# Small expert passes in raw fp32: 64 stationary tokens on each of the two column halves

## The reference, cut to what matters

```python
def moe_swiglu(h, w_router, w1, w3, w2):
    logits = (h @ w_router).astype(jnp.float32)
    top_logit, top_idx = lax.top_k(logits, TOP_K)
    gates = jax.nn.softmax(top_logit, axis=-1)
    ...
    def expert_block(args):
        xblk, e = args
        return (jax.nn.silu(xblk @ w1[e]) * (xblk @ w3[e])) @ w2[e]
    ...
    return jnp.zeros_like(h).at[tok].add(yb * gate[:, None])
```

## Time and profile before

| | us |
|---|---|
| median of 3 runs (2659.92 to 2661.28) | 2660.08 |
| profiled execution, span and own time | 2660.3 |
| PE busy | 2579.5 (97%) |
| DVE busy | 1747.8 (66%) |
| ACT busy | 1376.6 (52%) |
| pass 0 (small), from PE's first product to pass 1's | 1664 to 1774 |
| passes 1 and 2 (wide) | 1774 to 2109.5 |
| passes 3 to 7 (small) | 2109.5 to 2633 |
| output rows, last scatter, final norm, output | 2633 to 2660.3 |

### The profile page before, as it was taken

One profiled execution on the slowest core, in us unless ns is written; L12 is line 12 of the kernel. 1 busy time (PEld: TensorE's weight loads), 2 busy tenths in 40 slices (PEclk: granted clock), 3 DMA queues, 4 the chain that ended last, 5 costly groups with the idle time before them and its releaser, 6 DMA issues. The chain is left out here.

```text
span 2660.3 us, 46550 instructions
## 1 busy us (share of the span) xinstructions
PE 2579.5 (97%) x18338; PEld 2049.6 (77%) x18338; DVE 1747.8 (66%) x2600; ACT 1376.6 (52%) x2029; POOL 0.2 (0%) x4
## 2 busy tenths in 40 slices
PE   8999999999999999999999999999999999999997
PEld 6787777888788888877877899678888866666665
DVE  4876575445422233357765667977659899898897
ACT  5534375223422222255344635765557777777775
POOL 0000000000000000000000000000000000000000
PEclk9999999999999999999999999999999999999998
DMA  7011274224222223210103455885569999999996
GB/s 292 2 51 33 79 262 152 95 95 167 80 95 95 95 95 131 102 68 2 51 33 127 161 184 195 347 365 206 206 247 344 363 404 423 417 422 417 416 422 277
DMA packets 74103, 533.20 MB, mean 200 GB/s; under 512 B 8128, under 2 KB 9536, under 8 KB 9536
## 3 DMA queue, kind: packets, MB, share of 16 engines
q1 hardware_dynamic: 73632, 528.84, 51.3%
q10 hardware_dynamic: 288, 1.74, 0.2%
HBM read 529.50 MB, written 1.05 MB: 199 GB/s over the span
## 5 line engine op out<-in xcount | busy, mean ns | idle before, releaser
L1711 ACT ACTIVATE arena<-bank 128x512 f32<-128x512 f32 (+6 forms) x564 | 267.0, 489 | 724.6 <-PE bank L610 651.5
L1711 ACT ACTIVATE weights_high<-ring 128x1024 fp32r<-128x1024 f32 (+1 forms) x332 | 442.8, 1342 | 269.7 <-PE bank L610 255.7
L2533 DVE TENSOR_TENSOR weights_low<-ring,weights_high 128x1024 fp32r<-128x1024 f32 x220 | 266.8, 1224 | 400.6 <-ACT weights_high L1711 400.5
L610 PE MATMUL bank<-h_low,weights_high 128*128 128x512 f32 (+1 forms) x960 | 347.3, 362 | 0.0
L2930 DVE TENSOR_TENSOR weights_low<-ring,weights_high 128x2048 fp32r<-128x2048 f32 x112 | 255.7, 2286 | 53.5 <-ACT weights_high L1711 53.2
L610 PE MATMUL bank<-arena 64*64 64x64 f32 (+5 forms) x4944 | 266.9, 242 | 15.6 <-DVE arena L2748 4.5
L610 PEld LDWEIGHTS bank<-arena 64*64 64x64 f32 (+3 forms) x4944 | 224.5, 143 | 39.1 <-issue 13.9
L610 PEld LDWEIGHTS bank<-h_low,weights_high 128*128 128x128 f32 x960 | 182.0, 190 | 27.3
L2930 DVE TENSOR_TENSOR more_weights_low<-arena,weights_high 128x2048 fp32r<-128x2048 f32 x78 | 178.3, 2286 | 30.3 <-ACT weights_high L1711 29.5
L610 PE MATMUL bank<-h_high_gates,weights_high 128*128 128x512 f32 (+1 forms) x512 | 173.1, 338 | 4.3 <-DVE weights_low L2533 3.6
L610 PE MATMUL bank<-h_high_ffn,weights_high 128*128 128x512 f32 x448 | 175.7, 392 | 1.4 <-DVE h_low L2540 0.8
(11 more groups left out here) (384 smaller groups left out, 5123.0 us busy)
## 6 DMA issues: line engine op xcount, KB each, us to landing
ring<-wstream SPq DMA_DIRECT2D x345, 1024.0 KB, 5.2
arena<-wstream SPq DMA_DIRECT2D x153, 1024.0 KB, 8.3
xT<-xin SPq DMA_DIRECT2D x2, 1024.0 KB, 6.2
cn<-consts SPq DMA_DIRECT2D x1, 1576.0 KB, 21.2
sm<-small SPq DMA_DIRECT2D x1, 1568.0 KB, 23.6
sm<-small ACTq DMA_DIRECT2D x1, 1568.0 KB, 10.8
out<-hT SPq DMA_DIRECT2D x2, 512.0 KB, 3.0
cn<-consts ACTq DMA_DIRECT2D x1, 130.0 KB, 3.0
```

The costliest lines, as they stand in the source:

```text
L610: return nc.tensor.matmul(o, lhsT, rhs, start=first, stop=last)
L1711: return nc.scalar.activation(o, i, func, **kw)
L2533: step(vx.tensor_tensor(ring_low[:, u % RING, cols], ring[:, u % RING, cols], wh[:, j % 4, :].bitcast(F32), ALU.subtract), "weights low", j)
```

## The change

In small passes no unit is split, and neither are tokens and hidden. The 64 slots are one fp32 stationary operand of 64 columns (`xs`, `gs`), and `small_unit` multiplies a raw unit with four matmuls: of an inner unit the even k-tiles go to output rows 0 to 63 and the odd ones to rows 64 to 127, which is the left and the right half of the array's columns; of a down unit the two hidden tiles do. The two halves of the rows are then partial sums, and the steps that added them before add them still. The hidden is turned from its 64 rows alone. `first_high`, `next_high` and the low parts for a small pass are gone; a wide pass after a small one still gets its first three units copied, which ACT does when they have landed. At the end three units of a pass that may not come are loaded, instead of four. Wide passes are as before.

```diff
-UNSPLIT = [2] + list(range(7, 2 * PAIRS, 4)) + [33, 38]
-SPLIT = [q for q in range(MOE_UNITS) if q not in UNSPLIT]
...
+        xs = nc.alloc_sbuf_tensor_at("tokens", [P, KD, SMALL], F32, offset=tile_at(8))
+        gs = nc.alloc_sbuf_tensor_at("hidden", [P, FT, SMALL], F32, offset=tile_at(14))
...
-            begun = SPLIT[AHEAD - 1] + 1
+            begun = AHEAD
...
+                def small_unit(q, factors):
+
+
+                    pe.wait_ge(moe_loaded[q % MOE_RING], i * (16 * MOE_UNITS // MOE_RING) + 16 * (q // MOE_RING + 1))
+                    for o, left, cols, first, last in factors:
+                        ins = mm(o, left, moe_slot(q)[0][:, cols], first, last)
+                    ins.then_inc(*tick(moe_used, kind, "spent", q))
+
                 def by_unit(q, factors, low_done, more=(), more_room=()):
...
-                    if not wide:
-                        for o, left, cols, first, _ in factors:
-                            mm(o, left[0], high[:, cols], first, False)
-                        pe.wait_ge(*low_done)
-                        for o, left, cols, _, last in factors:
-                            ins = mm(o, left[0], low[:, cols], False, last)
-                        return ins.then_inc(*tick(moe_used, kind, "spent", q))
...
+                        o, h = bank[5 - 3 * (p % 2)][:, c * P:c * P + to.stop], ghid[to, p % 2, c * P:(c + 1) * P]
+                        ins = nc.tensor.transpose(o, h, C("ident")) if wide else mm(o, h, C("ident", SMALL)[to, :])
...
+                            small_unit(q, [(bank[3 + p % 2][rows(k), :], xs[:, 4 * b + k, :], slice(k * TOK, (k + 1) * TOK),
+                                            b == 0 and k < 2, b == 1 and k >= 2) for k in range(4)])
...
+                        small_unit(2 * PAIRS + q, [(bank[6 + n][rows(c), :], gs[:, 2 * q + c, :],
+                                                    slice(c * D + n * 512, c * D + n * 512 + 512), q == 0, q == PAIRS - 1)
+                                                   for n in range(2) for c in range(2)])
...
-            first_high(AHEAD - 1)
...
                 def next_high(q):
 
-                    u = split_units(wide_next)[q]
-                    act.wait_ge(moe_loaded[u], (i + 1) * (16 * MOE_UNITS // MOE_RING) + 16)
-                    act.wait_ge(*here("spent", split_units(wide)[q - AHEAD]))
-                    f(moe_high(q), moe_slot(u)[0], ACT.Copy).then_inc(*tick(e_scalars, kind, "next high", q))
+                    if not wide_next:
+                        book.leave_out(e_scalars)
+                        return
+                    act.wait_ge(moe_loaded[q], (i + 1) * (16 * MOE_UNITS // MOE_RING) + 16)
+                    if wide:
+                        act.wait_ge(*here("spent", MOE_UNITS + q - AHEAD))
+                    f(moe_high(q), moe_slot(q)[0], ACT.Copy).then_inc(*tick(e_scalars, kind, "next high", q))
...
-                    if l and t == KD - 2:
-                        dve.wait_ge(*done("first high", 0))
-                        rest(0)
...
                 for q in range(AHEAD - 1):
+                    if not wide_next:
+                        book.leave_out(e_vectors)
+                        continue
                     dve.wait_ge(*here("next high", q))
-                    rest(split_units(wide_next)[q], q).then_inc(*tick(e_vectors, kind, "next low", q))
+                    rest(q).then_inc(*tick(e_vectors, kind, "next low", q))
```

More of the change, by code:

```diff
@@ L505, in in_pass @@
             return s, (i + 1) * per_pass(s) + value
-        BOUNDARY = [("y kept", 0), ("y kept", 1), ("gathered low", 0), ("gathered low", 1)] + \
+        BOUNDARY = [(name, b) for name in ("y kept", "gathered kept", "gathered low") for b in range(2)] + \
             [(name, q) for name in ("next high", "next low") for q in range(AHEAD - (name == "next low"))]
@@ L1530, in before, with hidden_ready @@
                     return in_pass(i - 1, *step)
+                def hidden_ready(p):
+                    return here("hidden low" if wide else "hidden kept", p)
+                def small_unit(q, factors):
[3 more added lines that the diff above has]
+                    ins.then_inc(*tick(moe_used, kind, "spent", q))
                 def by_unit(q, factors, low_done, more=(), more_room=()):
                     low = moe_slot(q)[1]
[L1536 to L1549 removed]
+                    high = moe_high(q)
+                    pe.wait_ge(*(here("high", q) if q >= AHEAD else before("next high", q)))
                     for o, left, cols, first, _ in factors:
@@ L1590, in expert_pass @@
                         if q == 0:
-                            pe.wait_ge(*before("gathered low", 1))
+                            pe.wait_ge(*before("gathered low" if wide else "gathered kept", 1))
                             if full:
@@ L1646, in expert_pass @@
                     if q == 0:
-                        pe.wait_ge(*here("hidden low", PAIRS - 5))
+                        pe.wait_ge(*hidden_ready(PAIRS - 5))
                         if full:
@@ L2333, in expert_pass @@
                     next_high(q)
-                act.wait_ge(*here("next high", AHEAD - 1))
-                f(es[:, 3:4], V("eps"), ACT.Copy)
+                act.wait_ge(*(here("next high", AHEAD - 1) if wide_next else here("y high", 1)))
+                f(es[:, 3:4], V("eps"), ACT.Copy).then_inc(*tick(e_scalars, kind, "pass left"))
                 pass_end(e_scalars, kind)
@@ L2925, in attention, with rest @@
                         weights_low(LAYER_START[l] + min(weights_due(l, n), GATE_AT + 4))
-            def rest(q, turn=None):
+            def rest(q):
                 raw, low = moe_slot(q)
-                return vx.tensor_tensor(low, raw, moe_high(q if turn is None else turn).bitcast(F32), ALU.subtract)
+                return vx.tensor_tensor(low, raw, moe_high(q).bitcast(F32), ALU.subtract)
             def scaled_router():
@@ L3092, in _ @@
             step(pick_tokens(0, False), "first picked")
-            vx.memset(ptg[:, :].bitcast(F32), 0.0)
-            for q in range(1, AHEAD - 1):
-                dve.wait_ge(*done("first high", q))
-                rest(q)
-            for b in range(2):
-                dve.wait_ge(*done("first kept", b))
-                step(vx.tensor_tensor(xh[:, 4 * b:4 * b + 4, SMALL:SLOTS],
-                                      bank[b][:, 0:4 * SMALL].rearrange("p (k t) -> p k t", k=4),
-                                      xh[:, 4 * b:4 * b + 4, 0:SMALL].bitcast(F32), ALU.subtract), "first low", b)
+            step(vx.memset(ptg[:, :].bitcast(F32), 0.0), "slot rows cleared")
             own()
-            dve.wait_ge(*done("first high", AHEAD - 1))
             dve.sem_inc(e_vectors, per_pass(e_vectors))
@@ L3233, in low @@
                     dve.wait_ge(*here("high", q))
-                    rest(q, high_turn(q, wide)).then_inc(*tick(e_vectors, kind, "low", q))
+                    rest(q).then_inc(*tick(e_vectors, kind, "low", q))
                 def add_last(g):
```

120 lines of the change are left out of this document (50 added, 70 removed).

## The result

| | median, us | lowest to highest | runs |
|---|---|---|---|
| before | 2660.0 | 2658.4 to 2661.3 | 4 |
| with the change | 2637.8 | 2636.0 to 2639.6 | 4 |
| with the change, a second time | 2636.7 | 2635.5 to 2639.1 | 4 |

The ratio to the kernel before is 0.9913, with an interval of 0.990 to 0.9925 (the second time 0.9907, 0.989 to 0.9923, against 2660.8). Faster by 22 us; the forecast was 2636.4.

The account below looks back on a forecast made before the run. The prediction took DMA to bound four small passes, PE passes 1 and 2, and the split to count only in pass 0, pass 3's front and the tail. 13.4 + 3.2 + 7.1 = 23.7 us gave 2636.4 us, range 2626 to 2646.

Parts of the forecast that it names:

- What bounds the passes: Small passes: DMA alone sets four of them, 2.50 us per unit; the split counts in pass 0, pass 3's front, the tail.
- PE per unit: PE in small passes: a changed unit takes 0.86 us with halves side by side, 1.71 us in turns.
- Rival 3: Small passes: PE becomes the bound, with halves in turns and a low clock, about 3050 us; chance 0.04.
- Start of pass 0: Before pass 0's first product: a subtraction and the tokens' low half fall away, 0.8 and 0.6 us gained.
- Pass 0: First small pass: loading resumes at 1664.6 us at the saturated rate, last unit lands at 1754.6, 13.4 us gained with the start.
- Pass 0 to pass 1: From pass 0's last unit to pass 1: copy, subtraction, rows and hand-over take 10.0 us, against 10.1 before.
- So nothing is given back: Boundary from pass 0 to pass 1: the 13.4 us gained by then stay.
- The clock: Small passes and tail: PE half idle may lose full clock; passes stay under 105 us, tail's unit 0.9 us more, 2637.3.
- Passes 1, 2 and 3: Passes 1 and 2 are PE's, gain 0; pass 3 rises from 406 to 419 GB/s, gain 3.2 us.
- passes 4 to 7: Last four small passes: gain 0, because DMA is full.
- rival 1: Small passes: DMA gets faster once ACT and DVE leave the weights alone, 12.9 us more, 2623.5 us; chance 0.09.
- Tail: From pass 7's last unit to the last scatter: 3.6 us instead of 10.7, through ACT's and DVE's rows, gain 7.1 us.

Follow-up runs that it names:

- half loads: Changed kernel, with passes 3 to 7 loading only the first half of each weight unit and multiplying it twice: 2570.0 us (one run).
- the warm end: Changed kernel with one loop, rows between the copies, 12 + 6 added matmuls after pass 0, 8 + 4 + 4 + 4 at the end: 2628.7 us.

## Why the prediction was right, step by step

*What bounds the passes.* "In four of them nothing but DMA counts": right. 42 loads of 1 MB (44.0 million bytes) at 422 GB/s are 104.4 us, passes with half the products keep that time, and passes with half the loads leave it. "75 us of 105" for PE's units before is 33 x 1.81 + 9 x 3.41 = 90 us, and 102 with its other work; "36 + 14 = 50 us" after is 90: the factor of two in a raw unit, as the runs with 12 raw units and with half loads show. The sum didn't notice, as 90 is still under 104.4. For pass 0 the record blamed the split's path through ACT, DVE and PE. That reading failed too: PE was busy for 106.6 of 110 us, and its waits for DVE's low parts come to 2.7 us of the 103 from 1665 to 1768. With 12 raw units, so with three fewer to copy and subtract, pass 0 took 2.8 us more: 112.5 us from its first product to pass 1's (1661.52 to 1774.04) for 109.7 (1664.65 to 1774.34). So it was mostly PE's products that set pass 0, and it gains because PE's work falls from 102 to 90 us.

*PE per unit.* "If they run side by side": right, and worth 72 us of PE's time per pass. Both ends of the bound were mispriced: 0.86 and 1.71 us were written, and 1.71 and 3.41 measured. With it falls "either value is under 2.50 us, and the choice moves only the tail": in turns the kernel is 337 us slower than before. Rival 3 asked for two failures where the first alone was enough, so its chance was put too low.

*Start of pass 0.* 1.7 for 1.4. DMA resumes 2.13 us after the first product (1659.74 to 1661.87) where 1.35 was said: the unit's price again.

*Pass 0.* 9.8 for 12.0. The rate is the saturated one, as forecast, but for the first loads. Missing are 0.8 us at the start (above) and 1.4 behind it: from the resumed issue to the last unit's products it is 91.4 us, not 90.0. By the transfers' records the first load lands 5.4 us after its issue (5.0 forecast), the other 34 take 85.9 us (85.0 forecast, as two of the first three come 0.4 to 0.6 us late), and PE takes up the last one 0.1 us after it has landed.

*Pass 0 to pass 1.* The chain was right to 0.2 us (9.8 for 10.0). The step that failed is "So nothing is given back": what stands behind the chain runs at half clock, which costs 2.4 us (1.6 in the second execution). "The clock" looked for this loss in the tail and in the passes, where PE's waits are 0.55 us and the clock stays at 1.00, not at the boundary, where PE waits 2.55 and 2.17 us. The Trainium skill ("TensorE: Matmul & The Clock Gate", HAM oscillation) warns of matmul bursts between waits for DMA, and has a case with long bursts that keeps the clock. The boundary agrees with the warning (clock 0.50 after a wait of 2.55 us), and passes 3 to 7 are like the long bursts: 0.55 us of waiting in each 2.49, and the clock at 1.00. The forecast had put them under the warning because it took PE for half idle.

*Passes 1, 2 and 3.* 0 for passes 1 and 2 is right to 0.1 us. By the transfers' records the last unit of pass 2 lands 12.5 us earlier than before, that of pass 3 14.9 and that of pass 7 17.9. So pass 3 gains 2.4 us for 3.2, and *passes 4 to 7* gain 3.0 for 0: "0, DMA is full" gave away the difference between 419 and 422 GB/s, 105 x (1 - 419 / 422) = 0.75 us per pass. It isn't rival 1: before reaches 422 in good stretches too,

```profile
2242.00:2292.00 50.00, 49.77 (x210) 34.12 (x209) 46.07 (x52) 40.05 (x49) 0.00 (x0) 1.00 1.01 422
```

so ACT and DVE don't slow the transfers. Before, PE and DVE, each within some us of the limit, sometimes freed a slot late; that is argued from the rows, no run took it apart.

*Tail.* 3.4 + 1.2 for 7.1. The step that failed is the path: the forecast led it through ACT's and DVE's rows, and PE's idle time of the earlier trace rows, put down to DVE's rows, hid a jump of 5 us that already ended last. After the change PE reaches the jump sooner, 1.10 us after the last unit was taken up instead of 5.41, and the jump takes 0.95 us longer: 3.4 us are left. Without the jump it is 3.70 us, for 3.6 forecast, but that is luck in part: the last unit's products took 1.94 us where 0.2 + 0.86 + 0.17 was said, and one half of DVE's rows was enough, 0.75 us, where both were counted, 1.4. After the scatter, 1.2 us came that the sum left out. ACT's last copy for the pass that never comes (2637.16, 1.91 us) had also held back the squares for the final norm: they started 1.5 us after the first residual (2640.43 to 2641.91) and start 0.5 us after it now (2618.70 to 2619.22).

So the total was right in good part because errors cancelled: 9 us too much in pass 0 (2.2), at the boundary (2.2), in pass 3 (0.8) and in the tail (3.7), against 8 too little at the start (0.3), in passes 4 to 7 (3.0), behind the scatter (1.2) and in a profiled execution of before that had lost 3.2 us to the clock. Behind that loss the two traces differ by 19.3 us, and by 20.8 with the second execution of the changed kernel. Whether the executions without a profile lost as much there isn't known; the medians differ by 22.2 us. The terms of the stated range add up to 7.8 and 9.4 us, where 9.6 and 10.4 were used; the result lies within either.

## What to carry to other kernels

Count instructions per unit of work from a group's total over a whole pass, not from a burst in the timeline, above all where one line of the program can issue two; a price off by two can hide for as long as something else sets the time, and takes every "it would still fit" with it. When work is cut from beside a saturated queue, the gain lies at the ends of the saturated stretch, and what is late next there can stand in no engine's row: here a jump, and the clock after a longer wait. A view names one releaser; where two waits end within half a microsecond, as DVE's rows and the jump did before the change, look at both. Look behind the last wait for both, and test a margin by halving the load of whatever sets the time, which shows how far the next limit is away.

## What the runs showed of the hardware

- An fp32 product in this trace is two matmul instructions of 0.43 us per 512 columns each; two column halves with moving data of their own ran side by side at no loss (89.7 against 161.7 us per pass, which is 1.71 us less for each unit of 3.41).
- On PE a branch to the head of a loop or out of its end took 0.08 to 0.25 us, one over the block of passes that don't run 5.0 us before and 5.9 us after the change; on ACT and DVE such a jump took 0.05 and 0.06 us. The views of PE show the wait as "issue" or under another releaser.
- The core drew 422 GB/s through the passes from 2201 us on, with ACT and DVE busy 21 us of 105; before, with both busy 80 to 92% of the time, good stretches had 422 as well.
- Where the granted clock falls to its lower level differs between executions of the same instructions: the same residual ahead of pass 0 came at 1645.09 us before, at 1641.91 and 1640.15 in the two executions of the changed kernel and at 1639.65 in that with the warm end. Totals that lie within 2 us need the trace to tell them apart.
